# Six U slots, ten V slots, a written-out last phase and three small zero matmuls per group in a decoder trunk with expert retrieval

## The reference

```python
def peer(xn, w_q, sub_keys, u_tab, v_tab):
    q = (xt @ w_q).reshape(t, PEER_HEADS, 2, PEER_HALF)
    s = jnp.einsum("thpd,hpnd->thpn", q, sub_keys).astype(jnp.float32)
    ...                       # top 16 of 16 x 16 candidates for each of 8 heads
    g = jax.nn.softmax(top_s, axis=-1).astype(xn.dtype)
    ...
    def chunk(args):
        xc, ic, gc = args
        u = jnp.take(u_tab, ic, axis=0)
        a = jnp.einsum("cd,chkd->chk", xc, u)
        w = gc * jax.nn.gelu(a, approximate=False)
        vv = jnp.take(v_tab, ic, axis=0)
        return jnp.einsum("chk,chkd->cd", w, vv)
```

## Time and profile before

| | us |
|---|---|
| median of 3 runs | 1776.74 (1758.18 to 1788.58) |
| profiled execution, its own time | 1772.18 |
| its span | 1770.3 |
| TensorE matmul busy | 1290.0 |
| VectorE busy | 1136.0 |
| GpSimd busy | 1021.6 |
| ScalarE busy | 452.2 |

### The profile page before, as it was taken

The page is one execution under the profiler, slowest core; times in us unless marked ns, Lnnn a source line. Parts: engine busy times, 40 slices in busy tenths (PEclk is TensorE's granted clock), DMA queues, the critical chain, the costliest instruction groups (busy, mean ns, idle before and its releaser), DMA issues.

```text
span 1770.3 us, 15245 instructions
## 1 busy us (share of the span) xinstructions
PE 1290.0 (73%) x4350; PEld 769.3 (43%) x4350; DVE 1136.0 (64%) x2583; ACT 452.2 (26%) x1372; POOL 1021.6 (58%) x1035
## 2 busy tenths in 40 slices
PE   8988567887785777776887489775678866666663
PEld 7876344544451563343444265434345422222221
DVE  3255798887765645648878736672888865444446
ACT  0212133333332112332323212341233421111111
POOL 0013656666556555766666636573666676666664
PEclk9999878898897888788888789787898888888887
DMA  9526989999999999999999989998999999999997
GB/s 333 178 107 237 337 333 363 385 387 379 369 391 345 351 357 387 364 364 387 402 402 401 389 315 345 331 354 323 354 405 363 362 384 381 376 366 371 365 366 279
DMA packets 224519, 619.19 MB, mean 350 GB/s; under 512 B 18945, under 2 KB 90683, under 8 KB 224443
## 3 DMA queue, kind: packets, MB, share of 16 engines
q0 software_dynamic: 147456, 536.94, 79.6%
q1 hardware_dynamic: 76987, 81.36, 14.0%
HBM read 617.17 MB, written 1.05 MB: 349 GB/s over the span
## 4 chain that ended last, share of the span: by engine, by line
PE 24%; DVE 20%; POOL 17%; issue 17%; another core or an unknown queue 9%; DMA 7%; ACT 5%; SPq 0%; DVEq 0%; POOLq 0%; ACTq 0%
PE tile L789 12%; DVE u_ring L1037 10%; PE acc L819 9%; POOL v_ring L570 9%; POOL u_ring L570 8%; DMA u_ring<-in_peer_u_dram,idx_all 5%; DVE xres L1064 3%; DMA v_ring<-in_peer_v_dram,idx_all 2%; ACT diag L631 2%; ACT gelus L625 1%; PE tile L924 1%; PE tile L955 0%; PE tile L951 0%; ACT L698 0%
## 5 line engine op out<-in xcount | busy, mean ns | idle before, releaser
L819 PE MATMUL acc<-v_ring,diag 128*128 128x512 f32 x1572 | 755.5, 636 | 151.8 <-issue 99.6
L1037 DVE CUSTOM_DVE_ANT_0 u_ring<-u_ring,xf 128x1024 f32<-128x1024 f32 x512 | 614.8, 1217 | 274.4 <-DMA u_ring<-in_peer_u_dram,idx_all 238.4
L570 POOL DMA_INDIRECT v_ring<-in_peer_v_dram,idx_all x512 | 514.0, 1004 | 435.1 <-PE acc L819 217.8
L570 POOL DMA_INDIRECT u_ring<-in_peer_u_dram,idx_all x512 | 505.9, 988 | 299.2 <-issue 149.6
L819 PEld LDWEIGHTS acc<-v_ring,diag 128*128 128x128 f32 x1572 | 314.3, 205 | 564.9 <-issue 556.5
L789 PE MATMUL tile<-w_ring,fT 128*128 128x256 f32 x480 | 148.2, 477 | 25.8 <-DVE fT L1183 18.0
L1064 DVE SCALAR_TENSOR_TENSOR xres<-v_ring,gelus,xres 128x1024 f32<-128x1024 f32 x119 | 152.7, 1283 | 14.7 <-DMA v_ring<-in_peer_v_dram,idx_all 13.3
L617 ACT ACTIVATE gelus<-dots 128x8 f32<-128x8 f32 x64 | 13.4, 209 | 526.1 <-issue 340.6
L789 PEld LDWEIGHTS tile<-w_ring,fT 128*128 128x128 f32 x480 | 118.3, 253 | 49.3 <-DVE fT L1183 19.9
L924 PE MATMUL tile<-keysT,pq 128*128 128x128 f32 x128 | 33.0, 401 | 144.0 <-ACT pq L728 80.4
L631 ACT ACTIVATE diag<-ident,gelus 128x128 f32<-128x128 f32 x393 | 121.8, 388 | 2.1
(11 more groups left out here) (167 smaller groups left out, 1002.9 us busy)
## 6 DMA issues: line engine op xcount, KB each, us to landing
w_ring<-in_peer_wq_dram SPq DMA_DIRECT2D x23, 1024.0 KB
w_ring<-in_w_out_dram SPq DMA_DIRECT2D x12, 1024.0 KB
w_ring<-in_w_kv_dram SPq DMA_DIRECT2D x12, 1024.0 KB
u_ring<-in_peer_u_dram,idx_all POOLq DMA_INDIRECT x512
v_ring<-in_peer_v_dram,idx_all POOLq DMA_INDIRECT x512
w_ring<-in_w_in_b_dram SPq DMA_DIRECT2D x8, 1024.0 KB
u_ring<-in_w_in_a_dram SPq DMA_DIRECT2D x4, 1024.0 KB, 12.8
w_ring<-in_w_mem_kv_dram SPq DMA_DIRECT2D x4, 1024.0 KB
```

The costliest lines, as they stand in the source:

```text
L570: pool.indirect_dma_start(ring[:, s, :], None, rows_[:, :], bass.IndirectOffsetOnAxis(idx_all[:, col:col + 1], 0), element_offset=(ph // 2 ...
L819: ins = pe.matmul(acc[:, 512 * n:512 * n + 512], diag[:, par * G + s, :], v_ring[:, s, 512 * n:512 * n + 512], start=(first and s == 0), s ...
L1037: dve.tensor_tensor_reduce(u_ring[:, s, :], u_ring[:, s, :], xf[:, :], 1.0, 0.0, ALU.mult, ALU.add, dots[:, par * G + s:par * G + s + 1])\
```

## The change

It has three parts.

1. `u_ring` gets six slots and `v_ring` ten; the memory is the same. Slots no longer coincide with a row's place in its group, so `u_place` and `v_place` give the slot and the count of the landing semaphore. U row n waits for dot n - 6, V row n for row n - 10. In the steady part the order on GpSimd stays V row n, U row n + 8. At the start it is six U rows, two V rows, four U rows; at the end it is adapted in the same way.
2. The loop of the last phase is written out on all engines.
3. In every group but the first of a phase TensorE does three matmuls of 64 columns, with the identity as weights and zeros as data, added to the first 64 columns of `acc`. They stand ahead of the group's sum and behind its side steps, and wait for 1, 3 and 5 dots of the group.

```diff
+NZERO = 64
+STEP_DOTS = [1, 3, 5]
...
+NU, NV = 6, 10
...
+def u_place(q, s):
+
+    return (G * q + s) % NU, 16 * ((G * q + s) // NU + 1)
+
+
+def v_place(q, s):
+    return (G * q + s) % NV, 16 * ((G * q + s) // NV + 1)
...
-        u_ring = sb("u_ring", [P, G, D])
-        v_ring = sb("v_ring", [P, G, D])
+        u_ring = sb("u_ring", [P, NU, D])
+        v_ring = sb("v_ring", [P, NV, D])
...
+                if n >= NU:
+                    pool.wait_ge(dot_done, n - NU + 1)
                 else:
-                    filled(pool, LAST_USE[HELD[s // 2]])
+                    filled(pool, LAST_USE[HELD[n // 2]])
...
-            for q in range(last):
-                if q == last - 1:
-                    for s in range(G):
-                        gather_u(last, s)
-                for s in range(G):
-                    gather_v(q, s)
-                    if q < last - 1:
-                        gather_u(q + 1, s)
-            for s in range(G):
-                gather_v(last, s)
+            early = G - NU
+            total = G * NQ
+            for n in range(NU):
+                gather_u(n)
+            for n in range(early):
+                gather_v(n)
+            for n in range(NU, NU + 2 * early):
+                gather_u(n)
+            for n in range(early, total - 2 * G):
+                gather_v(n)
+                gather_u(n + G)
...
-            def group(q, par, first=False):
+            def group(q):
+                for n in STEP_DOTS if q % GROUPS else []:
+                    pe.wait_ge(dot_done, G * q + n)
+                    pe.matmul(acc[:, 0:NZERO], ident[:, :], zeros[:, :], start=False, stop=False,
+                              skip_group_check=True)
                 for n_, s in enumerate(summed(q)):
                     pe.wait_ge(diag_made, sums_before(q) + n_ + 1)
-                    pe.wait_ge(v_landed[s], 16 * q + 16)
+                    at, landed = v_place(q, s)
+                    pe.wait_ge(v_landed[at], landed)
...
-            with pe.Fori(1, GROUPS // 2 - 1) as i:
-                for par in range(2):
-                    group(i * 2 + (base + par), par)
-            for q in (LOOPED, LOOPED + 1):
-                group(q, q % 2)
```

More of the change, by code:

```diff
@@ L76, in summed @@
     return [s for s in range(G) if s not in folded(q)]
[L79 to L85 removed]
 def folds_before(q):
[L89 removed]
+    return sum(len(folded(n)) for n in range(q))
 def sums_before(q):
[L93 removed]
+    return sum(len(summed(n)) for n in range(q))
+def u_place(q, s):
+    return (G * q + s) % NU, 16 * ((G * q + s) // NU + 1)
+def v_place(q, s):
+    return (G * q + s) % NV, 16 * ((G * q + s) // NV + 1)
 ROUTE_PARTS = 2
@@ L376, in trunk @@
         stat = sb("stat", [P, 4])
+        zeros = sb("zeros", [P, NZERO])
         negmax = sb("negmax", [P, 2, 2])
@@ L565, in _, with gather @@
                                pattern=[[-1, P]], channel_multiplier=1).then_inc(consts_made, 1)
-            def gather(rows_, ring, q, s, landed):
+            def gather(rows_, row, q, s, landed):
                 ph, g = divmod(q, GROUPS)
@@ L608, in _ @@
+            for n in range(total - 2 * G + early, total):
+                gather_v(n)
         @block.scalar
         def _(act):
-            def group(q, par, ph, head):
-                gate = gates[:, :, :].rearrange("p a n -> p (a n)")
+            def group(q):
+                ph, g = divmod(q, GROUPS)
+                par = q % 2
                 act.wait_ge(dot_done, G * q + G)
-                act.wait_ge(gate_made[ph % 2], heads_ready(ph, head))
-                if not (isinstance(q, int) and q < 2):
+                act.wait_ge(gate_made[ph % 2], heads_ready(ph, g // 2))
+                if q >= 2:
```

189 lines of the change are left out of this document (78 added, 111 removed).

## The result

The changed kernel takes **1814.6 us** (median of four runs, 1813.2 to 1833.7), the kernel before beside it 1782.7 us (1758.2 to 1798.5). The ratio is 1.0257, 95% interval [1.0179, 1.0335]: slower by 2.6%, where 1757 us and a range of 1718 to 1803 had been forecast. The profiled run has a span of 1812.0 us (before 1770.3) at a granted clock of 0.855 (0.857).

The account below looks back on a forecast made before the run. The prediction took GpSimd's gathers as the bound, at most 401 GB/s, starved by late V-slot releases from TensorE. Terms -17 - 1 - 5 - 5 + 2 + 6 = -20 gave a median of 1757 us, range 1718 to 1803.

Parts of the forecast that it names:

- Ten V slots in the last phase, -18: Last phase: one of two GpSimd stalls per two groups goes, -17 us, and -1 for the groups around the loop.
- rival B: GpSimd's V-slot stalls: ten slots shift each by two rows and remove none; 1780 us, no change; chance 22%.
- Quiet stretches, -5: Quiet stretches, one GpSimd stall a group in 17 groups: ten V slots save 5 us, bounds 0 and -20.
- Mixed stretches, -15 for V and +10 for U: 530 to 830 and 970 to 1290 us: ten V slots save 15, six U slots cost 10, together -5 us.
- Rival D, 1819 us: Mixed groups: six U slots too few, 14 of 20 groups lose 5.2 us each; 1819 us, slower; chance 16%.
- the 30 of the forecast: Sign in 970 to 1290 us: VectorE's wait for U rows should stay below 30 us.
- Start, +2: Kernel start: U rows 6 and 7 now wait for the first two dots, +2 us, bounds 0 and 5.2.
- Zeros, +6: TensorE's 64-column zero matmuls delay bursts that follow straight on side steps: 10 mixed groups x 0.6, +6 us.
- Loop written out, 0: Last phase's loop: writing it out changes nothing, 0 us, bounds 0 and -5.
- Four theories: Whole kernel: forecast 40%, stalls only move 22%, transfers stay full 22%, six U slots too few 16%.

Follow-up runs that it names:

- e1: Changed kernel without its zero matmuls (six U and ten V slots, last phase written out): 1810.7 us, ratio 1.0162 to the kernel before.
- e16: Changed kernel without zeros, V gathers in phases 0 to 2 also waiting for the row eight before, as with eight slots: 1784.4 us, ratio 1.0183 to the kernel before.
- e4: Changed kernel without zeros, six U slots and eight V slots, two of the ten unused: 1778.9 us, ratio 0.9973 to the kernel before.
- e12: Changed kernel without zeros, six U and eight V slots, at most five gathers in flight: 1782.8 us, ratio 1.0134 to the kernel before.
- e2: Changed kernel with eight U and eight V slots, zeros kept, last phase written out: 1774.0 us, ratio 0.9995 to the kernel before.
- e3: Changed kernel with eight U and eight V slots and no zeros, only the last phase written out: 1771.2 us, ratio 0.9962 to the kernel before.
- e13: Changed kernel without zeros, GpSimd waiting before V row 5 for TensorE's transposed queries in groups with a route: 1778.1 us, ratio 1.0143 to the kernel before.
- e6: Changed kernel without zeros, six U and ten V slots, at most four gathers in flight: 1944.2 us, ratio 1.0904 to the kernel before.
- e7: Changed kernel without zeros, eight U and eight V slots, at most four gathers in flight: 1932.9 us, ratio 1.0851 to the kernel before.
- e8: Changed kernel without zeros, eight U and eight V slots, at most five gathers in flight: 1775.4 us, ratio 0.9949 to the kernel before.
- e17: Changed kernel without zeros, six U and ten V slots, measured again beside e18: 1796.9 us, ratio 1.0195 to the kernel before.
- e18: Changed kernel without zeros, six U and ten V slots, at most five gathers in flight, beside e17: 1783.1 us, ratio 1.0144 to the kernel before.

## Why the prediction was wrong, step by step

- **Ten V slots in the last phase, -18: failed.** I took one of two stalls to vanish because the first slot's release would have come by then. It had been held, and it was held again. The two stalls became two others of 6.0 us together, or one of 4.6 to 5.5 us in e1 and of 3.4 to 4.7 in e16. The sum of the stalls stayed (33.9 us, before 32.6); what sets it isn't shown. Two groups take 45.7 us. Measured: 0, which was the bound that I had named and rival B's claim. B was right about this phase's time.
- **Quiet stretches, -5: failed, and it decided the sign.** "Moving a single stall doesn't remove it, so of the bounds 0 and -20": I left out that moving it could cost. Measured +27 in groups 4 to 9, of which 9 were made up by group 16. The stall wasn't only a loss; it was the moment at which ScalarE and VectorE got their side steps' tiles. I had the evidence in hand, showed a query tile that ScalarE received 10 us late and just as GpSimd stood still, and I wrote of it "I don't know why" and then worked out every term as if releases kept time.
- **Mixed stretches, -15 for V and +10 for U: failed in the V part.** U alone: e4 is 0.9973 and its profile loses nothing there, so +10 looks too large, with the doubt that e12 and e16 leave. V: +25 in groups 23 to 27, by the held attention product.
- **Rival D, 1819 us: right number, wrong mechanism.** It said that VectorE would find too few rows and put more than 60 us of VectorE's waits between 970 and 1290 us as its mark. These waits are 24.8 us, under the 30 of the forecast, and e4 speaks against it. What D had right is that GpSimd would stop sooner for U slots: 198 us in place of 21.
- **Start, +2: as said.** The lag at group 3 is 0.4 us.
- **Zeros, +6: not contradicted.** e2 is 2.8 us slower than e3 by the medians and 5.8 by the means, inside both intervals. Three take 0.78 us in the place shown, 0.26 each, under the 0.36 from which I worked. In the last phase they leave the clock alone (0.861 in e2 and 0.862 in e3 from group 50 to 62), as forecast and for the reason given: they run at the end of the burst before. Over the whole run the granted clock is a little higher with them, 0.858 to 0.868 in e2's four executions against 0.851 to 0.856 in e3's; no time came of it.
- **Loop written out, 0: right**, e3 0.9962 [0.9924, 1.0001].
- **Chances.** Four theories, and none held a held release of a side step. B came next to it, with "a release comes through only once GpSimd has stopped issuing", and I priced B as no gain, without asking what stops when the stop goes.

## What to carry to other kernels

Before taking a stall away, list who gets something during it. Where an engine's waits end long after the instruction they are put down to, or on "remote", and again and again a few microseconds after another engine's last issue, that delay is a mechanism of the kernel, and a change that moves the stop has to be priced by it. If one part of a change only shifts a stop, bound it on both sides of zero. And an added wait can pay: one that stops the gathers for 2.5 us right behind a release on which three engines hang spared a stand of 8 us in e13's profile, though e13's ratio isn't told from e1's.

## What the runs showed of the hardware

- TensorE's semaphore updates often reach the other engines late while GpSimd issues gathers one after another: 8.1 us (297.84 to 305.93) and 14.2 us (804.67 to 818.89) in the changed kernel. They come in the order of TensorE's instructions, so that one can wait behind several (799.59 to 818.86). In the places shown they come 1.7 to 3.6 us after GpSimd's last issue, and 5.0 us after it in e1's last phase (1619.87 to 1624.89). Of the recorded updates for V slots 99.7% are on time with at most four gathers in flight (e6, e7) and 50 to 73% without a limit. VectorE's updates are hardly touched: 95% of those recorded for dots are on time before, 94% in the changed kernel.
- The trace itself loses updates where gathers are dense: of the 16 a gather gives on landing it holds 39% in the kernel before and 91% in e7. A missing update is no late one.
- With five of these 0.5 MB gathers in flight the rate from 280 to 530 us is 368 GB/s and the run takes 1775 us (e8); with four it is 325 GB/s and 1933 us (e7). From the end of an issue to the landing it was 5.1 us in the median of e7, over the 625 gathers whose landing is recorded in full. The Trainium skill (DMA: Bandwidth & Descriptors, section Anatomy of one DMA — SWDGE (gpsimd) path) has a fit by which such a gather would take an estimated 2.0 + 524288 / 436000 = 3.2 us alone; no gather is alone in these runs, and the measured 5.1 decides here.
- The same kernel, the one before, had medians from 1755 to 1786 us in five sessions, 1.8% apart; two of them, 1786 and 1764 us, were on the same chip. Ratios under that size need runs side by side, and e17 and e18 were worth more than all comparisons across sessions.
